# Three fp32r passes for the first slot of the feed-forward down projection, with the split of its inputs moved

## The reference

```python
def conv_ffn(h, w_up, dw_w, dw_b, w_down):
    u = dwconv(h @ w_up, dw_w, dw_b)
    a, g = jnp.split(u, 2, axis=-1)
    return (a * jax.nn.silu(g)) @ w_down
```

## Time and profile before

| | |
|---|---|
| median of three runs | 2339.55 us (2336.91 to 2339.84) |
| span of the profiled execution, first to last instruction | 2338.6 us |
| the profiled execution's own time | not listed apart from its span |
| mean granted TensorE clock | 0.985 |
| TensorE busy (PE) | 2279.2 us, 97% |
| VectorE busy | 1433.2 us, 61% |
| ScalarE busy | 979.4 us, 42% |
| GpSimd busy | 108.2 us, 5% |
| first down slot, layer 0 | 1567.50 to 1604.86 us |
| first down slot, layer 1 | 2269.27 to 2288.07 us |

### The profile page before, as it was taken

How to read it: one execution, slowest core, us unless ns; L and a number is a source line. 1 busy time by engine, 2 the same in 40 slices (tenths; PEclk the granted TensorE clock), 3 DMA queues, 4 the chain that set the end, 5 groups by cost and what they waited for, 6 DMA issues and landing times.

```text
span 2338.6 us, 35274 instructions
## 1 busy us (share of the span) xinstructions
PE 2279.2 (97%) x15026; PEld 1915.9 (82%) x15026; DVE 1433.2 (61%) x2626; ACT 979.4 (42%) x1587; POOL 108.2 (5%) x87
## 2 busy tenths in 40 slices
PE   6999999999999999999999999999999999999999
PEld 4898888978877887778887677876878878998999
DVE  1566744667648777546444556564277766676984
ACT  2447633367523345353222333330244545644542
POOL 0000000000000032120000000000000222100000
PEclk8999999999999999999999999999999999999999
DMA  9894257963535121113332555322332212564553
GB/s 303 256 293 149 94 179 254 297 209 107 163 110 162 36 73 37 46 45 114 102 108 90 166 176 167 121 86 81 104 110 75 89 55 73 171 203 142 186 173 118
DMA packets 335532, 322.99 MB, mean 138 GB/s; under 512 B 28560, under 2 KB 334992, under 8 KB 335248
## 3 DMA queue, kind: packets, MB, share of 16 engines
q1 hardware_dynamic: 335376, 320.74, 43.4%
HBM read 319.67 MB, written 1.05 MB: 137 GB/s over the span
## 4 chain that ended last, share of the span: by engine, by line
PE 89%; DVE 6%; DMA 2%; ACT 2%; issue 0%; POOL 0%; SPq 0%; DVEq 0%; ACTq 0%
PE ps L745 88%; DVE parts L2036 1%; DMA ring<-w_ada 1%; ACT w_high L1504 1%; DMA ring<-w_in 1%; PE ps L1258 1%; DVE arena L2580 1%; DVE parts L2394 0%; DVE arena L2181 0%; POOL parts L1961 0%; DVE arena L2175 0%; SPq L676 0%; ACT arena L1620 0%; DVE arena L2130 0%; DVE arena L2423 0%
## 5 line engine op out<-in xcount | busy, mean ns | idle before, releaser
L745 PE MATMUL ps<-parts,w_high 128*128 128x256 f32 (+1 forms) x6512 | 1152.2, 326 | 3.2 <-ACT w_high L1504 2.1
L745 PEld LDWEIGHTS ps<-parts,w_high 128*128 128x128 f32 x6512 | 969.3, 189 | 130.2 <-issue 23.2
L745 PE MATMUL ps<-parts,parts 128*128 128x256 f32 (+1 forms) x3384 | 607.7, 321 | 4.5 <-DVE parts L2394 2.6
L1504 ACT ACTIVATE w_high<-ring 128x1024 fp32r<-128x1024 f32 (+2 forms) x442 | 439.7, 1011 | 321.5 <-PE ps L745 246.2
L745 PEld LDWEIGHTS ps<-parts,parts 128*128 128x128 f32 x3384 | 504.7, 190 | 57.0 <-DVE parts L2394 3.1
L2394 DVE TENSOR_TENSOR parts<-ring,w_high 128x1024 fp32r<-128x1024 f32 (+2 forms) x282 | 319.9, 1141 | 190.5 <-ACT w_high L1504 190.3
L745 PE MATMUL ps<-arena 128*64 128x256 f32 (+7 forms) x928 | 183.7, 396 | 11.9 <-ACT arena L1591 9.0
L1961 POOL TENSOR_TENSOR parts<-ring,w_high 128x512 fp32r<-128x512 f32 x80 | 107.4, 1368 | 1891.3 <-ACT w_high L1504 1891.2
L745 PEld LDWEIGHTS ps<-arena 128*128 128x128 f32 (+2 forms) x928 | 122.2, 170 | 60.1 <-issue 19.9
L2423 DVE SCALAR_TENSOR_TENSOR arena<-arena,cols 128x512 f32<-128x512 f32 (+1 forms) x240 | 159.5, 664 | 6.2
L2036 DVE TENSOR_TENSOR parts<-ring,w_high 128x1024 fp32r<-128x1024 f32 x88 | 103.7, 1220 | 91.5 <-ACT w_high L1504 91.5
(11 more groups left out here) (272 smaller groups left out, 1811.8 us busy)
## 6 DMA issues: line engine op xcount, KB each, us to landing
ring<-w_in SPq DMA_DIRECT2D x118, 1024.0 KB, 5.3
ring<-ada_w SPq DMA_DIRECT2D x48, 1024.0 KB, 5.4
ring<-ffn_w_up SPq DMA_DIRECT2D x44, 1024.0 KB, 5.1
ring<-w_ada SPq DMA_DIRECT2D x24, 1024.0 KB, 7.4
ring<-w_out SPq DMA_DIRECT2D x16, 1024.0 KB, 5.2
ring<-ffn_w_down SPq DMA_DIRECT2D x16, 1024.0 KB, 5.3
ring<-w_out SPq DMA_DIRECT2D x16, 512.0 KB, 4.5
ring<-w_mlstm_out SPq DMA_DIRECT2D x8, 1024.0 KB, 5.1
```

The lines of the kernel that those rows point to most:

```text
L745: return tensor.matmul(o, a, b, start=first, stop=last)
L1504: scalar.activation(half_high(m), half_raw(m), ACT.Copy).then_inc(*a.step(("w_high", m)))
```

## The change

The first slot is made in three passes like the others, in both layers. So it has six more weight halves to split and needs both parts of all activation tiles. Three things move with it:

- The low parts of its weights are made by GpSimd (`down_lows`), two instructions for each half.
- The activation parts are made by a new helper `act_split`, cast and difference together, two tiles at a time, right behind the products; it no longer waits for the first slot's results.
- In layer 0, six of the tiles (`ACT_AHEAD`) are split one by one during slots 4 to 9 of the up projection. The high parts of tiles 0 to 5 lie in a space of their own behind `h_high["up"]`, in both layers. In layer 1 nothing is split ahead.

```diff
-    if name[0] == "down" and name[2]:
+    if name[0] == "down":
         return "down", name[1]
...
+ACT_AHEAD = 6
...
+        high_ahead = under([P, ACT_AHEAD, TT], FREE_AT + KT * TT)
...
+        def act_high(t):
+
+            return high_ahead[:, t, :] if t < ACT_AHEAD else h_high["down"][:, t, :]
...
                         for j in range(2):
-                            if s:
-                                name = ("down", l, s, part)
-                                i = split_strip(us[j][:, lo:TT], name, j, lo, act_low, part * KT, part == 0, part == 2)
-                                names = [("used_half", half_no[name, j])] + ([("used", name)] if j else []) + ([("full", ("down", l, 2 * s + j))] if part == 2 else [])
-                                i.then_inc(*pe.step(*names))
-                                continue
-                            for k in range(nk):
-                                kk = part * 8 + k
-                                pe.wait_ge(*when(("act", l, kk)))
-                                i = mm(us[j][:, lo:TT], wt[:, k, j * P:(j + 1) * P], act[:, kk, lo:TT], kk == 0, kk == FT - 1)
...
+                            name = ("down", l, s, part)
+                            i = split_strip(us[j][:, lo:TT], name, j, lo, act_low, part * KT, part == 0, part == 2, high=[act_high(part * KT + k) for k in range(nk)])
...
+            def down_lows(l):
+
+                first = half_no[("down", l, 0, 0), 0]
+                for n in range(first, first + 6):
+                    p.wait_ge(*when(("w_high", n)))
+                    nk = half_size(n)[0] // 2
+                    for part in (slice(0, nk), slice(nk, 2 * nk)):
+                        gpsimd.tensor_tensor(half_low(n)[:, part, :], half_raw(n)[:, part, :], half_high(n)[:, part, :].bitcast(F32), ALU.subtract).then_inc(*p.step(("w_low", n)))
+
             for l in range(DEPTH):
                 back_lows(l)
+                down_lows(l)
...
+                    if l == 0 and 0 <= s - 4 < ACT_AHEAD:
+                        act_split(l, [s - 4], lo)
                 for j in range(2):
                     product(l, 10, j, lo)
 
+                first_half = half_no[("down", l, 1, 0), 0]
                 v.wait_ge(*when(("act", l, FT - 1)))
-                for t in range(FT):
-                    v.wait_ge(*when(("act", l, t)))
-                    vector.tensor_copy(h_high["down"][:, t, lo:TT], act[:, t, lo:TT]).then_inc(*v.step(("h_high", "down", l, t)))
-                first_half = half_no[("down", l, 1, 0), 0]
+                for t in range(0 if l else ACT_AHEAD, FT, 2):
+                    act_split(l, [t, t + 1], lo)
                 for m in range(SPLIT_BUFS):
                     low_part(first_half + m)
-                v.wait_ge(*when(full(("down", l, 1))))
-                for t in range(FT):
-                    v.wait_ge(*when(("h_high", "down", l, t)))
-                    vector.tensor_tensor(act_low[:, t, lo:TT], act[:, t, lo:TT], h_high["down"][:, t, lo:TT].bitcast(F32), ALU.subtract).then_inc(*v.step(("h_low", "down", l, t)))
...
+            def act_split(l, tiles, lo):
+
+                for t in tiles:
+                    v.wait_ge(*when(("act", l, t)))
+                    vector.tensor_copy(act_high(t)[:, lo:TT], act[:, t, lo:TT]).then_inc(*v.step(("h_high", "down", l, t)))
+                for t in tiles:
+                    v.wait_ge(*when(("h_high", "down", l, t)))
+                    vector.tensor_tensor(act_low[:, t, lo:TT], act[:, t, lo:TT], act_high(t)[:, lo:TT].bitcast(F32), ALU.subtract).then_inc(*v.step(("h_low", "down", l, t)))
```

More of the change, by code:

```diff
@@ L612, in program @@
         upc = Ff(2, 2, 2, TT)
-        assert Ff.at == FREE_AT and FREE_AT + KT * TT <= N_ARENA
+        assert Ff.at == FREE_AT and FREE_AT + (KT + ACT_AHEAD) * TT <= N_ARENA
+        def act_high(t):
+            return high_ahead[:, t, :] if t < ACT_AHEAD else h_high["down"][:, t, :]
         sems = {k: ctx.enter_context(nc.semaphore(k + "_steps")) for k in ("pe", "act", "dve", "pool")}
@@ L1420, in second_layer @@
                         for j in range(2):
-                            if s:
-                                name = ("down", l, s, part)
-                                i = split_strip(us[j][:, lo:TT], name, j, lo, act_low, part * KT, part == 0, part == 2)
-                                names = [("used_half", half_no[name, j])] + ([("used", name)] if j else []) + ([("full", ("down", l, 2 * s + j))] if part == 2 else [])
-                                i.then_inc(*pe.step(*names))
-                                continue
-                            for k in range(nk):
-                                kk = part * 8 + k
-                                pe.wait_ge(*when(("act", l, kk)))
-                                i = mm(us[j][:, lo:TT], wt[:, k, j * P:(j + 1) * P], act[:, kk, lo:TT], kk == 0, kk == FT - 1)
[L1431 to L1434, removed]
+                            name = ("down", l, s, part)
+                            i = split_strip(us[j][:, lo:TT], name, j, lo, act_low, part * KT, part == 0, part == 2, high=[act_high(part * KT + k) for k in range(nk)])
+                            names = [("used_half", half_no[name, j])] + ([("used", name)] if j else []) + ([("full", ("down", l, 2 * s + j))] if part == 2 else [])
+                            i.then_inc(*pe.step(*names))
             for l in range(DEPTH):
```

## The result

The changed kernel takes 2358.49 us (median of 4, 2355.66 to 2361.42) against 2338.61 for the kernel before in the same comparison: ratio 1.0082, 95% interval 1.0070 to 1.0094. It is slower by 19.9 us; the forecast was 2362 and slower. The profiled span is 2357.1 us, against 2338.6.

What follows compares the result with a forecast made beforehand. TensorE was taken to bound the kernel (89% of the span), with time lost by any wait put before it. Layer 0 +6.9, layer 1 +13.2 and clock +3 gave +23, 2362 us, range 2343 to 2373.

Steps and rivals of the forecast that it cites:

- TensorE's own work: First down slot in three passes: 30.6 us in layer 0, 15.7 in layer 1; work alone -9.9 us.
- The start: At the slot's start TensorE waits for ScalarE's first high behind gates(10): 4.6 us in layer 0, 3.5 in layer 1.
- the prediction's third rival: Faster: no wait at the slot's start and parts keep pace, so the 9.9 us come through, 2330 us; chance 0.03.
- Turns: First down slots: each VectorE cast or subtraction waits for one GpSimd instruction, priced as both alone summed; +6.9 and +13.2 us.
- The taps of rows 5: Profiled VectorE taps beside GpSimd: 1.45 us a turn against 1.58 summed, so up to 1 us less in layer 1.
- the highs up to tile 15: Layer 0, half 2: activation highs ready about 1594 us, after three more pairs and four short GpSimd instructions, 9.4 us.
- tile 7's high in layer 1: Layer 1, half 0: the highs of tile 7 were forecast ready at about 2285.6 us, its low at 2286.2.
- Clock: Granted clock falls to 0.50 after TensorE stalls in the first slots; +3 us, bounds 0 and 7.
- three stalls: TensorE stalls at the start and middle of layer 0's slot and start of layer 1's; what falls under the first is hidden.
- Edits at nothing: Extra highs, ScalarE's new wait, SyncE's weight loads and later slots were taken to cost nothing.
- Side by side: First slots: casts and subtractions don't exclude GpSimd; +2.3 us, 2342, with clock 2342 to 2346; chance 0.14.
- VectorE first: First slots: GpSimd gets nothing until VectorE's parts are done; +14.4 and +13.9 us, with clock 2371; chance 0.10.

Runs made afterwards that it cites:

- e8: Kernel before with only layer 0's first slot in three passes: highs early, lows on VectorE, TensorE's passes reordered by tile groups; 2332.23 us, ratio 0.9965.
- e5: Changed kernel with ScalarE making the highs of down halves 0 and 1 earlier, ahead of gates(10), GpSimd's lows kept; 2348.57 us, ratio 1.0038 to before.
- e7: Changed kernel with layer 1 plain, highs early, all lows on VectorE, pass order kept; 2336.13 us, ratio 0.9986 to before.
- e3: Changed kernel with GpSimd's lows writing 8 columns per tile instead of 128, TensorE using highs in their place; 2343.31 us, ratio 1.0016 to before.
- e4: Changed kernel with the six low weight halves a layer made by VectorE between activation parts instead of GpSimd; 2343.22 us, ratio 1.0021 to before.
- e10: Changed kernel with unused plain products filling TensorE's long waits, run again beside the unaltered changed kernel; 2351.19 us, ratio 1.0053 to before.
- e9: The changed kernel unaltered, run again on the same chip as the one with filled waits; 2360.75 us, ratio 1.0088 to before.
- e1: Changed kernel with the change in layer 0 only, layer 1's first slot plain; 2346.61 us, ratio 1.0029 to before.
- e12: Changed kernel with GpSimd's lows started only after VectorE cast tile 8 (layer 0) or 2 (layer 1); 2356.80 us, ratio 1.0076 to before.

## Why the prediction was right

- **What bounds it.** Right: the slots were covered before, and the time is the TensorE waits put into them.
- **TensorE's own work.** 30.6 us for the slot in three passes in layer 0: e8 has 30.6.
- **The start.** 4.6 and 3.5 us forecast, 4.58 and 3.66 measured. In layer 1 the wait ended with VectorE's first cast; the prediction named ScalarE's high alone, which came at almost the same time. That the wait isn't removed by earlier highs, since tile 6 (tile 0 in layer 1) comes at about the same time, e5 and e7 show; the prediction's third rival named the late high as the only condition beside the parts keeping pace. e8 met both in layer 0.
- **Turns.** The mechanism is shown by e3 and e4. The price was high by an eighth: a pair was to take 6.86 us in layer 0 and took 6.13, in layer 1 6.05 against 2286.36 - 2281.02 = 5.34. A turn is shorter than the sum of both alone, 1.53 us against 1.71 in layer 0. The taps of rows 5 showed this already: the prediction set their 1.45 beside 1.24 + 0.34, but a tap alone takes 1.04 / 2 = 0.52, so the sum to compare is 1.76. Worked through in its own terms, two steps also come later than it says: the highs up to tile 15 at 1586.4 + 9.4 - 1.2 = 1594.6, not about 1594, and tile 7's high in layer 1 at about 2286.1, not 2285.6. So its sum would have been some 1 us higher, and the turns 3 us too dear instead of 2. Slots with the clock held (e10): +6.1 and +11.9, forecast +6.9 and +13.2.
- **Clock.** Forecast +3 between 0 and 7; 4.3 in the slots by e10. The prediction counted three stalls and thought the first hidden. So it was: the first product behind layer 0's second stall comes 23.3 us after TensorE's arrival in the changed kernel (1588.02 - 1564.70) and in e10 alike; behind it e10 is 2.3 us shorter. In layer 1 it is 2.0.
- **Edits at nothing.** Right as far as the trace shows: later slots keep 5.57 and 2.85 us a strip, and between and behind the slots the time fell by 1.1 us rather than grew.
- **Rivals.** Side by side would have given 2342 to 2346, which is what the kernel takes once GpSimd's work is gone (e3). VectorE first was given 0.10 and does occur, for instructions that come late (below), but in the changed kernel not for the first half of either layer, where it counts.

Two errors, -2.1 in the turns (18.0 against 20.1) and +1.3 in the clock, partly cancel, which is luck: 22.4 us in the slots against the 23 of the sum. The profiled span grew by 18.5 only, mostly because TensorE came earlier to the first slot in that execution. In e9, the same kernel with slots of the same length, it came 3.1 us later than in the kernel before and the span is 24.1 us longer. The timed 19.9 lies between.

## What to carry to other kernels

An engine that sits idle isn't free help if its instructions and those of the engine it helps hold each other up: look in the trace for a place where both work on SBUF, and read what one instruction of each takes there. Before a covered stage is made shorter, list what it covers and when each input of the new form is ready; here 9.9 us of products saved brought 8.2 us of new waits (4.58 + 3.66) before any contention. When an input comes late, first try to order the consumer's work by what is ready: in layer 0 the same three passes lost 7.7 us in e1 and gained 7.5 in e8, with early highs, no GpSimd, and TensorE's order changed. In layer 1 no form tried beat the plain slot.

## What the runs showed of the hardware that was not expected

GpSimd and VectorE don't always take turns. In e12, layer 1, GpSimd's first instruction began inside a run of casts and subtractions and was done only when the run was over, while VectorE went on at its own length. GpSimd's and then VectorE's rows of the timeline of e12:

```profile
2280.16 12.81 POOL L1971 TENSOR_TENSOR parts<-ring,w_high 128x512 fp32r<-128x512 f32 x2 [270.69 <-DVE parts L2792]
...
2280.87 0.48 DVE L2792 CAST parts<-arena 128x256 fp32r<-128x256 f32 x2
2281.28 0.75 DVE L2795 TENSOR_TENSOR parts<-arena,parts 128x256 fp32r<-128x256 f32 x2
```

Two instructions took 12.81 us, of which the second is 1.3. In e5, layer 0, three short ones took 11.76 us, of which the first is 9.8:

```profile
1578.51 11.76 POOL L1970 TENSOR_TENSOR parts<-ring,w_high 128x384 fp32r<-128x384 f32 x3 [4.75 <-ACT w_high L1500]
```

But in e12, layer 0, GpSimd also began inside such a run and got its turn at once, ten in 15.01 us, while two subtractions took 3.43:

```profile
1577.42 15.01 POOL L1971 TENSOR_TENSOR parts<-ring,w_high 128x512 fp32r<-128x512 f32 x10 [532.73 <-DVE parts L2792]
...
1577.59 3.43 DVE L2795 TENSOR_TENSOR parts<-arena,parts 128x512 fp32r<-128x512 f32 x2
```

In the rows here, once turns had begun, they went on as long as GpSimd had a next instruction waiting. What decides which of the two happens when it comes in stays open. The Trainium skill, SBUF — State Buffer, section Who interferes with whom, has the port pair that VectorE and GpSimd share held for a whole instruction by whoever issues first. That agrees with the turns in the main; one of them took 1.53 us, a little less than the 1.71 of both one after the other. In layer 1 of e12 GpSimd waited not for one instruction of VectorE's but for some forty.
